# Products that nobody reads on TensorE through fox, mlstm and parts of HGRN, and half of a convolution on GpSimd

## The reference

```python
def fox_mixer(q, k, v, fz, gain):            # 4 heads of 64, causal
    cum_logf = jnp.cumsum(jax.nn.log_sigmoid(fz), axis=1)
    s = q @ k.T * scale + fq[..., None] - cum_logf[:, :, None, :]
    p = jax.nn.softmax(jnp.where(causal, s, NEG_BIG), axis=-1)
    out = p @ v

def mlstm_mixer(q, k, v, o, ig, fz, conv_w, gain):
    qk = jax.nn.silu(causal_depthwise_conv(jnp.concatenate([q, k], axis=-1), conv_w))   # 4 taps, 512 channels
    qk_c = q_c @ k_c.T * exp(d_log - m_t)    # decayed scores, then times v

def _hgrn2_chunk(state, inp):                # chunks of 64 positions
    scores = jnp.einsum('bhtk,bhsk,bhtsk->bhts', q, k, decay)
    o_intra = jnp.einsum('bhts,bhsv->bhtv', scores, v)
```

## Time and profile before

| | |
|---|---|
| median of 3 executions | 1773.51 us (1773.16 to 1774.23) |
| profiled execution, its own time | 1772.93 us |
| span of that execution | 1771.1 us |
| mean granted clock of TensorE | 0.92 |
| busy share of the span | TensorE 91%, VectorE 47%, ScalarE 31%, GpSimd 15% |
| TensorE instructions | 7372 |
| fox | 1139.6 to 1200.2 |
| mlstm | 1200.6 to 1255.7 |
| HGRN's levels | 1255.9 to 1302.7 |

### The profile page before, as it was taken

One profiled execution on the slowest core, in us unless ns is written; L12 is line 12 of the kernel. 1 busy time (PEld: TensorE's weight loads), 2 busy tenths in 40 slices (PEclk: granted clock), 3 DMA queues, 4 the chain that ended last, 5 costly groups with the idle time before them and its releaser, 6 DMA issues. The chain is left out here.

```text
span 1771.1 us, 18376 instructions
## 1 busy us (share of the span) xinstructions
PE 1619.4 (91%) x7372; PEld 1297.5 (73%) x7372; DVE 828.3 (47%) x1217; ACT 553.8 (31%) x839; POOL 261.3 (15%) x275
## 2 busy tenths in 40 slices
PE   7987999678988899999997999999868899999997
PEld 6875777566767788888886766765757688888886
DVE  4233333446654444434336666644664533323434
ACT  4221333424442432222224213334123422212222
POOL 0000000000020697000002466000320100000000
PEclk9999999889998999999998999855759899999999
DMA  4222111220022223222231222200002222222222
GB/s 163 96 92 74 48 48 60 72 72 1 1 71 84 75 102 102 102 97 95 95 119 33 95 72 72 79 0 1 1 1 71 72 95 95 95 95 95 97 85 92
DMA packets 34633, 129.23 MB, mean 73 GB/s; under 512 B 4548, under 2 KB 18780, under 8 KB 22132
## 3 DMA queue, kind: packets, MB, share of 16 engines
q1 hardware_dynamic: 34260, 127.93, 21.1%
q10 hardware_dynamic: 288, 0.12, 0.0%
HBM read 124.82 MB, written 3.17 MB: 72 GB/s over the span
## 5 line engine op out<-in xcount | busy, mean ns | idle before, releaser
L223 DVE TENSOR_TENSOR ring_lo<-ring_raw,ring_hi 128x2048 fp32r<-128x2048 f32 (+5 forms) x115 | 266.7, 2322 | 218.5 <-ACT ring_hi L213 218.4
L242 PE MATMUL bank<-xT_hi,ring_hi 128*128 128x512 f32 (+1 forms) x864 | 342.7, 397 | 5.1 <-PEq L1257 3.4
L242 PE MATMUL bank<-xT_hi,ring_lo 128*128 128x512 f32 (+1 forms) x864 | 338.8, 392 | 0.0
L242 PE MATMUL bank<-xT_lo,ring_hi 128*128 128x512 f32 (+1 forms) x864 | 338.8, 392 | 0.0
L213 ACT CAST ring_hi<-ring_raw 128x2048 fp32r<-128x2048 f32 (+5 forms) x115 | 212.7, 1852 | 270.4 <-DMA ring_raw<-in_w_ff 131.1
L242 PEld LDWEIGHTS bank<-xT_hi,ring_hi 128*128 128x128 f32 (+1 forms) x864 | 163.4, 189 | 44.6 <-issue 10.0
L242 PEld LDWEIGHTS bank<-xT_hi,ring_lo 128*128 128x128 f32 (+1 forms) x864 | 162.8, 188 | 35.6
L242 PEld LDWEIGHTS bank<-xT_lo,ring_hi 128*128 128x128 f32 (+1 forms) x864 | 163.1, 189 | 34.3
L242 PE MATMUL bank<-ring_hi,hid_hi 128*128 128x512 f32 x432 | 169.9, 393 | 4.0 <-DVE ring_lo L223 4.0
L242 PE MATMUL bank<-ring_lo,hid_hi 128*128 128x512 f32 x432 | 169.4, 392 | 0.0
L242 PE MATMUL bank<-ring_hi,hid_lo 128*128 128x512 f32 x432 | 169.3, 392 | 0.0
(11 more groups left out here) (440 smaller groups left out, 2297.4 us busy)
## 6 DMA issues: line engine op xcount, KB each, us to landing
ring_raw<-in_w_ff SPq DMA_DIRECT2D x32, 1024.0 KB, 4.8
ring_raw<-in_w_up SPq DMA_DIRECT2D x22, 1024.0 KB, 4.9
ring_raw<-in_w_proj SPq DMA_DIRECT2D x8, 1024.0 KB, 5.2
ring_raw<-in_w_gates SPq DMA_DIRECT2D x8, 1024.0 KB, 4.9
ring_raw<-in_w_out SPq DMA_DIRECT2D x8, 1024.0 KB, 4.9
ring_raw<-in_w_fm SPq DMA_DIRECT2D x12, 512.0 KB, 4.5
ring_raw<-in_w_dn_a SPq DMA_DIRECT2D x6, 1024.0 KB, 4.9
ring_raw<-in_w_proj SPq DMA_DIRECT2D x8, 512.0 KB, 4.6
```

The source lines that it names most:

```text
L223: k.nc.vector.tensor_tensor(k.ring.lo[:, g % SLOTS, 0:n], k.raw[:, g % SLOTS, 0:n], plain(k.ring.hi[:, g % SLOTS, 0:n]), ALU.subtract).the ...
L242: mm = k.nc.tensor.matmul(out, x, y, start=first and n == 0, stop=last and n == 3 * len(pairs) - 1)
```

## The change

A helper `keep_busy(k, n)` issues n products of 128x512 in bf16 (an identity matrix by a mask) into PSUM bank 7. Nothing reads that bank. They are issued:

- 10 at the end of the projections' block, behind a wait for the last of the four gates of `S5Glu`;
- in fox 8 ahead of round 0 and 2 in each of the 18 rounds, after the scores and before the transposes; 44 in all;
- in mlstm 2 after the scores of each of the 16 pieces; 32 in all;
- in HGRN 3 at level 0 and 6 at each of the levels 6 to 9, ahead of the scores; 27 in all.

That makes 113. Beside it the convolution is divided. Tiles 0 and 1 stay on VectorE in rounds 0 and 1. Tiles 2 and 3 go to GpSimd, which starts with fox: for each a multiplication, then three times a multiplication into a scratch tile (2 KB per partition at 178 KB) and an addition, each waiting for the one before, 14 instructions in all. ScalarE's sigmoids are taken in round 4 (tiles 0 and 1) and in round 10 (tiles 2 and 3), and VectorE's multiplications by them in rounds 7, 8, 13 and 14. The other callers of `stage_attention` pass no `busy`, and their GpSimd program is empty.

```diff
+def keep_busy(k, n):
+    for _ in range(n):
+        k.nc.tensor.matmul(k.pb[7][:, :], k.identb[:, :], k.mask_lev[:, 0:4, :].rearrange("p t s -> p (t s)"),
+                           start=True, stop=True)
...
+            if busy:
+                keep_busy(k, 4 * busy)
             for i in range(nb + 2):
                 if i < nb:
                     scores(i)
                     if beside is not None:
                         beside.pe(pe, i)
+                keep_busy(k, busy)
                 if 1 <= i <= nb:
                     turn(i - 1)
...
+        @block.gpsimd
+        def _(pool):
+            if beside is not None:
+                beside.pool(pool)
...
             glu.products(pe)
+            pe.wait_ge(glu.gate.sem, glu.gate.base + T)
+            keep_busy(k, 10)
...
+    def pool(self, pool):
+        k, g, cv = self.k, self.k.nc.gpsimd, self.k.conv
+        link = Chain(pool, k.sig("pool_chain"))
+        for f in (2, 3):
+            x, z = k.fm[:, 10 + f, :], self.part
+            link(g.tensor_scalar(cv[:, f, :], x, col(k, "conv_w", 4 * f + 3), None, ALU.mult))
+            for i in (1, 2, 3):
+                link(g.tensor_scalar(z[:, 0:S - i], x[:, 0:S - i], col(k, "conv_w", 4 * f + 3 - i), None, ALU.mult))
+                y = g.tensor_tensor(cv[:, f, i:], cv[:, f, i:], z[:, 0:S - i], ALU.add)
+                if i < 3:
+                    link(y)
+            y.then_inc(self.pooled.sem, 1)
+
     def act(self, act, r):
-        if r == 5:
-            for f in range(4):
-                act.wait_ge(self.summed.sem, self.summed.base + f + 1)
+        if r in (4, 10):
+            for f in (0, 1) if r == 4 else (2, 3):
+                s = self.summed if f < 2 else self.pooled
+                act.wait_ge(s.sem, s.base + f % 2 + 1)
...
     def dve(self, dve, r):
         k, v, cv = self.k, self.k.nc.vector, self.k.conv
-        if r < 4:
+        if r < 2:
...
-        elif 8 <= r < 12:
-            f = r - 8
+        elif r in (7, 8, 13, 14):
+            f = (7, 8, 13, 14).index(r)
...
-    stage_attention(k, batches, 1.0, 158, beside=Convolution(k))
+    stage_attention(k, batches, 1.0, 158, beside=Convolution(k), busy=2)
...
                     for u in range(T):
                         scores(4 * h + u)
+                        keep_busy(k, 2)
...
                     pe.wait_ge(zr.sem, zr.base + i)
+                keep_busy(k, 3 if i == 0 else 6 if i >= 6 else 0)
                 for h in range(4):
```

More of the change, by code:

```diff
@@ L661, in sync @@
         issue_chunks(self.k, sp, self.end + SLOTS)
+    def pool(self, pool):
+        pass
     def pe(self, pe, r):
@@ L702, in close, with stage_attention @@
         self.free.base += len(self.steps)
-def stage_attention(k, batches, scale, bufs_kb, lse=None, beside=None):
+def stage_attention(k, batches, scale, bufs_kb, lse=None, beside=None, busy=0):
     nc = k.nc
@@ L2274, in __init__ @@
         self.cs = k.sb("convs", 40, [P, 4, S])
-        self.summed, self.sigmoid = k.sig("conv_summed"), k.sig("conv_sigmoid")
+        self.part = k.sb("conv_part", 178, [P, S])
+        self.summed, self.pooled, self.sigmoid = k.sig("conv_summed"), k.sig("conv_pooled"), k.sig("conv_sigmoid")
     def sync(self, sp):
@@ L2309, in close @@
     def close(self):
-        self.summed.base += 4
+        self.summed.base += 2
+        self.pooled.base += 2
         self.sigmoid.base += 4
```

## The result

The changed kernel takes 1801.9 us in the median of four executions (1799.2 to 1802.8), the kernel before 1773.7. The ratio is 1.0157, 95% interval 1.0139 to 1.0174. The profiled execution has a span of 1800.3 us against 1771.1, 29.2 more.

A forecast was written before the change was run, and what follows sets the result against it. TensorE at the low clock was taken to bound fox and mlstm. The terms 2.0 + 1.8 + 5.1 + 9.1 + 9.4 + 0 = +27.4 on 1772.93 gave 1800.3, said as 1800 us, range 1789 to 1805.

The forecast's parts named there:

- C: Fox's first rounds: VectorE and GpSimd hold each other up in the divided convolution, +5.1 us, bounds -2 and +7.
- E: mlstm: five rounds' products hidden, eleven rounds of two pay 0.427 each, +9.4 us; bounds +5.0 and +13.7.
- A: End of the projections: ten products wait for ScalarE's last gate and delay the block's end, +2.0 us.
- B: Ahead of fox's round 0: eight products that nothing covers, +1.8 us.
- The step on which all hangs: Fox rounds 0 and 1: TensorE waits 3 to 4 us of each 6, so the clock falls again and stays low.
- Rival 1: Fox: the clock falls but comes back midway with the added products; 1782 us, chance 0.12.
- D: Fox rounds 4 to 17, low clock: products +10.3 us, filling the gap at ScalarE's sigmoids -1.2; +9.1 in the sum.
- F: HGRN: products hidden beside VectorE or, at level 9, costing up to 2.6 us or bringing 1.2; taken as 0.
- Rivals 2 and 3: Clock holds through fox and goes in mlstm (1768 us, chance 0.18), or holds in both stages (1747 us, chance 0.10).
- rival 2: Clock holds through fox if VectorE's tile stays under some 3.5 us: fox 45.6 us instead of 60.5; chance 0.18.

The follow-up runs named there:

- no_products: The changed kernel without any of its 113 products, only the convolution divided between VectorE and GpSimd: 1773.9 us, ratio 1.0001 to the kernel before.
- spread_two: Kernel before with the convolution dealt out over fox's rounds on VectorE, 10 and 8 products at the seam, two per fox round: 1763.7 us, ratio 0.9947.
- conv_on_dve: The changed kernel with its 113 products, but the convolution as before, four tiles on VectorE in rounds 0 to 3: 1794.0 us, ratio 1.0116.
- filled: Kernel before with convolution dealt out on VectorE, 4 products at the seam, 1 to 5 per fox round, 67 in mlstm, none in HGRN: 1751.6 us, ratio 0.9873.
- four_a_round: conv_on_dve with four products in each of fox's rounds in place of two: 1780.8 us, ratio 1.0044 to the kernel before.
- no_fox_rounds: The changed kernel without the 2 products in each of fox's 18 rounds, the 8 ahead of round 0 kept: 1791.1 us, ratio 1.0099.
- spread_none: Kernel before with the convolution dealt out over fox's rounds on VectorE, no unread products anywhere: 1774.4 us, ratio 1.0002.

## Why the prediction was right, by its steps

The forecast of 1800 stands at 1801.9, and on the mechanism it gave: the clock falls again inside fox, does not come back there, and each product that TensorE can't hide costs 0.427. That the sum came within 2 us is in part luck: C was 2.7 us too high and E 3.8 too low. The range of 1789 to 1805 had left out E's own upper bound of 13.7, near which E came out; with it the range would have reached 1809.

- **A and B, the seam**, +3.8 forecast, +3.7 measured, and the same in all eight kernels with the 10 and 8.
- **C, the convolution**, was too high, +5.1 against +2.4. The step that failed is that each of VectorE's eight operations waits 0.6 to 1.0 for GpSimd. In the trace of after the two tiles last 4.0 and 4.2 us (the first from 1146.38 to 1150.41), not 5.5; a multiply-add that starts inside a GpSimd addition took 1.63 or 1.46, one that starts inside a multiplication 1.06 or an undisturbed 0.75. no_products has the term by itself, +2.2. And the clock stayed full to 1153.1, not to 1144. GpSimd's own bounds were wrong too, the other way: a multiplication of 512 columns took 1.57 us, above both rows that I took as its bounds (0.61 and 1.04), so the chain lasted 22 us and not 8.5 to 14.6. Nobody waited for it, since ScalarE asks for it in round 10.
- **The step on which all hangs** was right in its result, and its reason was mis-sized. It gave TensorE 3 to 4 us of waiting in each of rounds 0 and 1; in the trace of after TensorE waited once, for 1.76 us, between fox's first product and the fall (6.34 of 8.10 busy). Its comparison with before was misread: the 8.93 of 10.60 of the earlier trace rows lie behind the fall. Before, the clock fell some 1.5 us into fox, with TensorE busy 4.84 of 4.90, and what stood ahead was the 1.51 us of idle at the seam. That dealing out VectorE's block of tiles keeps the clock up is shown by spread_two beside conv_on_dve; that TensorE's waits are the link fits nearly all the falls read here, but is argued, since in filled the clock fell at 1218.5 with TensorE busy 37.66 of 37.70. The step's second half, that the clock doesn't come back, is a matter of how many products: two a round don't bring it back within the rounds, four do (four_a_round). Rival 1 had named the right force and lacked the amount.
- **D**, +9.1 against +8.3. The products cost 9.9 (58.70 against 48.85 in no_fox_rounds), where 10.3 was counted; 2.2 of the 3.4 us at the full clock from 1214.5 lie in this stretch. The other part, forecast at -1.2, was -1.6 (48.85 against 50.44), but for another reason: the 1.20 us of idle belong to VectorE's tiles, as the rows under no_products show, and not to ScalarE's sigmoids. That this part came out right is luck.
- **E, mlstm**, was mis-sized, +9.4 against +13.2. The step that failed reads five rounds' products as hidden in a gap that its own row gives as 1.59 us. Five rounds need 4.3 us; TensorE was busy 11.54 of 13.20 us in that window, so at most two rounds could hide, and in the trace of after ScalarE's block begins 7.5 us after mlstm's first product instead of 7.0, which takes part of these. The upper bound of the term, 13.7, was the better reading.
- **F, HGRN**, 0 forecast, -1.1 in the profile and nothing in the medians.
- Rivals 2 and 3 asked whether the clock holds when VectorE is not held by GpSimd. conv_on_dve answers no at two a round (1794, clock low from 1156.4): there VectorE's four whole tiles are enough to make it fall. With the tiles dealt out it does hold for most of fox, and rival 2's price for fox and seam, 45.6 us, is 3.4 below spread_two's 45.3 + 3.7 = 49.0.

## What to carry to other kernels

Unread products to hold a clock are a purchase: at the low clock each costs twice as much as at the full one, so a number that fails to hold it is the worst of all (the change's 113 cost 28 us; one a round in fox with an even VectorE gave 17 there and took 3.7 at the seam). First remove the wait that makes the engine pause, here by spreading another engine's block over the rounds, and then add the few products that bridge what is left. How few is open: no run has the even convolution with products at the seam and none in the rounds, or the reverse. When a gap is claimed as cover, compare the microseconds of the gap with those of the work, not the rounds that it spans.

## What was not expected of the hardware

A busy TensorE is not enough for the full clock. "Busy" is here the profile's own measure, in which the ends of matmuls are modelled. The granted clock stayed at 0.51 over 58.2 us in which TensorE was busy for 57.1, and in spread_none it fell and stayed low with 10.58 of 10.60 busy. In filled it fell at 1218.5 behind 37.7 us without a gap to speak of. The Trainium skill, "TensorE: Matmul & The Clock Gate", section "Why this matters for your kernels", advises to keep TensorE busy continuously to get the full clock; these rows don't agree. In four_a_round the clock came back within fox at nearly the same busy share (98% against conv_on_dve's 97%), with more products of `keep_busy` between the stage's own. GpSimd's multiplication by a scalar per partition (1.57 us for 512 columns) was slower than its addition of two tensors (1.08 when undisturbed), the reverse of what I had taken.
